# Block 1's linear attention: five levels and the diagonal as 32x32 blocks in a compact area

## The reference

```python
def gla_chunk_scan(q, k, v, log_g, state0, with_output):
    ...
    def step(state, inp):
        qc, kc, vc, gc = inp
        b = jnp.cumsum(gc.astype(jnp.float32), axis=2)
        ...
        diff = jnp.where(lower_tri, b[:, :, :, None, :] - b[:, :, None, :, :], -jnp.inf)
        a = jnp.einsum('bhtk,bhsk,bhtsk->bhts', qc, kc, jnp.exp(diff))
        o = (jnp.einsum('bhts,bhsv->bhtv', a, vc)
             + jnp.einsum('bhtk,bhkv->bhtv', qc * jnp.exp(b), state))
        return new_state, o
```

## Time and profile before

| what | value |
|---|---|
| median of three runs | 2466.95 us |
| span of the profiled execution | 2469.0 us |
| PE, PEld busy | 97%, 83% |
| DVE, ACT busy | 73%, 60% |
| layer 0: first diagonal product to first out-projection product | 219.47 to 268.36 us |
| layer 1: the same | 817.13 to 847.79 us |
| mean granted clock of PE | 0.993 |

### The profile page before, as it was taken

How to read it: one execution, slowest core, us unless ns; L and a number is a source line. 1 busy time by engine, 2 the same in 40 slices (tenths; PEclk the granted TensorE clock), 3 DMA queues, 4 the chain that set the end, 5 groups by cost and what they waited for, 6 DMA issues and landing times.

```text
span 2469.0 us, 38577 instructions
## 1 busy us (share of the span) xinstructions
PE 2402.1 (97%) x15096; PEld 2048.9 (83%) x15096; DVE 1803.2 (73%) x2445; ACT 1478.9 (60%) x1940; POOL 27.0 (1%) x86
## 2 busy tenths in 40 slices
PE   8999999999999899999999999999999999999998
PEld 6876788888887688898888889898888888888886
DVE  5556666566566666676666657579898898898997
ACT  4255366465444556556665545667777777777775
POOL 0000000000000000010000001000000000000000
PEclk9999999999999999999999999999999999999999
DMA  8236245555544545554235545147998998999996
GB/s 340 103 145 258 111 156 189 189 185 189 186 162 148 230 177 188 188 181 154 89 142 197 188 171 198 69 154 271 372 358 338 370 359 339 368 361 351 360 359 255
DMA packets 81640, 564.58 MB, mean 229 GB/s; under 512 B 9328, under 2 KB 12672, under 8 KB 13632
## 3 DMA queue, kind: packets, MB, share of 16 engines
q1 hardware_dynamic: 80144, 559.97, 60.6%
q0 software_dynamic: 1328, 2.25, 0.3%
HBM read 559.97 MB, written 1.05 MB: 227 GB/s over the span
## 4 chain that ended last, share of the span: by engine, by line
PE 88%; DVE 5%; ACT 4%; issue 1%; DMA 1%; SPq 0%; DVEq 0%; ACTq 0%
PE psum L247 86%; DVE ring_lo L241 2%; ACT ring_hi L238 2%; PE psum L740 1%; PE psum L2518 1%; DMA ring<-in_stream 1%; DMA Z<-in_first_mods 1%; ACT hT L793 1%; DVE hT L829 1%; ACT Z L801 0%; ACT turned_probs L801 0%; DVE hT L1533 0%; DVE Z L1465 0%; DVE mixT L647 0%; DVE hT L444 0%
## 5 line engine op out<-in xcount | busy, mean ns | idle before, releaser
L241 DVE TENSOR_TENSOR ring_lo<-ring,ring_hi 128x2048 fp32r<-128x2048 f32 x477 | 1092.2, 2291 | 272.7 <-ACT ring_hi L238 266.9
L238 ACT ACTIVATE ring_hi<-ring 128x2048 fp32r<-128x2048 f32 x477 | 912.4, 1914 | 334.1 <-PE psum L247 327.8
L247 PE MATMUL psum<-h_parts,ring_hi 128*128 128x512 f32 (+1 forms) x3184 | 861.2, 350 | 8.4 <-DVE h_parts L454 4.1
L247 PE MATMUL psum<-h_parts,ring_lo 128*128 128x256 f32 (+1 forms) x2464 | 601.6, 291 | 0.0
L247 PEld LDWEIGHTS psum<-h_parts,ring_hi 128*128 128x128 f32 x3184 | 515.8, 190 | 34.4 <-issue 10.5
L247 PE MATMUL psum<-ring_hi,h_parts 128*128 128x512 f32 (+1 forms) x1920 | 534.6, 365 | 0.4 <-ACT tok L324 0.4
L247 PEld LDWEIGHTS psum<-h_parts,ring_lo 128*128 128x128 f32 x2464 | 466.6, 189 | 72.5
L247 PEld LDWEIGHTS psum<-ring_hi,h_parts 128*128 128x128 f32 x1920 | 338.6, 189 | 52.6 <-ACT tok L324 0.8
L247 PE MATMUL psum<-ring_lo,h_parts 128*128 128x512 f32 (+1 forms) x960 | 347.5, 362 | 0.0
L247 PE MATMUL psum<-ring_hi,Zr 128*128 128x512 f32 (+1 forms) x736 | 225.3, 388 | 0.0
L247 PEld LDWEIGHTS psum<-ring_lo,h_parts 128*128 128x128 f32 x960 | 181.0, 189 | 28.8
(11 more groups left out here) (305 smaller groups left out, 2078.7 us busy)
## 6 DMA issues: line engine op xcount, KB each, us to landing
ring<-in_stream SPq DMA_DIRECT2D x524, 1024.0 KB, 4.8
Z<-in_first_mods SPq DMA_DIRECT2D x5, 1024.0 KB, 16.9
cst<-in_constants SPq DMA_DIRECT2D x1, 1216.0 KB, 7.9
mixT<-mixT POOLq DMA_DIRECT2D x32, 35.5 KB, 4.0
xT<-in_xT SPq DMA_DIRECT2D x1, 1024.0 KB, 6.2
xT<-in_ctxT SPq DMA_DIRECT2D x1, 1024.0 KB, 8.5
xT<-in_memT POOLq DMA_DIRECT2D x1, 1024.0 KB, 8.7
out_y<-hT SPq DMA_DIRECT2D x4, 256.0 KB, 2.5
```

Of the source, the lines that this page charges most:

```text
L238: e.activation(hi, raw, ACT.Copy).then_inc(sem("piece_rounded"), 1)
L241: e.tensor_tensor(lo, raw, hi.bitcast(F32), ALU.subtract).then_inc(sem("piece_split"), 1)
L247: ins = pe.matmul(*args, **kw)
```

## The change

Diagonal and levels 0 to 4 no longer multiply 128 by 128 but only the four 32x32 blocks on the diagonal of each tile and head (all that these five levels want lies there): 16 products of 32 keys by 32 queries for a tile instead of four. The results lie side by side in 64 columns of two banks for each tile, in turn in banks 2, 3 and 4, 5. DVE takes a level of all tiles and heads with one masked copy, 128 by 512 elements in layer 0 and 128 by 256 in layer 1, into a compact area `gA_blocks`, after the merges of that level. Levels 5 and 6 are multiplied as before, in banks 0 to 3; ACT copies them whole into `gA`, two tiles (one in layer 1) after each half of level 6; then DVE places the blocks over them, four copies of 32 partitions for each half. The merges of level 6 no longer have copies between them. `pe_gla_out` waits for all of this before its products with the values. ACT's split of two pieces comes after its copies of level 6. The masks shrink from 7x128 to 5x32 columns, and `other_w` gets memory of its own, so that POOL loads it without waiting for `keys_decayed`.

```diff
-        lvl_mask = sb("lvl_mask", [P, LEVELS, P], U8)
-        other_w = sb("other_w", [P, DEPTH, TAPS], over="lvl_mask")
+        lvl_mask = sb("lvl_mask", [P, BLOCK_LEVELS, BLOCK], U8)
+        other_w = sb("other_w", [P, DEPTH, TAPS])
...
+        gA_blocks = hflat[:, 2048:2560].rearrange("p (u w n) -> p u w n", u=2, n=BLOCK)
...
+        def pe_blocks(pe, i, tiles, keys_at, queries_at):
+
+            for t in tiles:
+                for c in range(2):
+                    at = 256 + (2 * t + c) * BLOCK
+                    for a in range(0, P, BLOCK):
+                        for u in range(2):
+                            r = slice(u * HD, (u + 1) * HD)
+                            mm(pe, bank[block_banks(i) + u][a:a + BLOCK, at:at + BLOCK],
+                               keys_at[r, c, t * P + a:t * P + a + BLOCK], queries_at(t, r, c, a), start=True, stop=True,
+                               last_of="grams" if (t, c, a, u) == (tiles[-1], 1, P - BLOCK, 1) else None)
+
         def pe_gla_levels(pe, layer):
...
+            for tiles in halves_of(nt):
+                pe_blocks(pe, 0, tiles, GK, lambda t, r, c, a: GQ[r, c, t * P + a:t * P + a + BLOCK])
+            phase_others(pe)
+            for l in range(BLOCK_LEVELS):
+                if l:
+                    pe.wait_ge(sem("gram_read"), rd + l)
+                for tiles in halves_of(nt):
+                    await_next(pe, "level_keys" if l else "level")
+                    pe_blocks(pe, l + 1, tiles, keys_now if l else GK, lambda t, r, c, a: queries_now(l, t, r, c, a))
                 for m in in_level(layer, l):
                     pe_mod_add(pe, layer, 1, m)
+            advance(pe, "level", 4 * (BLOCK_LEVELS - 1))
+            pe.wait_ge(sem("gram_read"), rd + BLOCK_LEVELS)
+            for l in range(BLOCK_LEVELS, LEVELS):
+                for tiles in halves_of(nt):
+                    await_next(pe, "level", 2)
+                    for t in tiles:
+                        pe_direct(pe, l, t, nt, t == tiles[-1])
...
         def act_gla_levels(act, layer):
...
-            for t in range(nt):
-                act.wait_ge(sem("grams"), gr + t + 1)
-                act.activation(by_bank(t), grams(t), ACT.Copy, scale=2.0).then_inc(sem("gram_read"), 1)
+            act.wait_ge(sem("grams"), gr + 2)
+            act.activation(blocks_kept(nt), block_grams(0, nt), ACT.Copy, scale=2.0).then_inc(sem("gram_read"), 1)
...
             act_rows_sum(act, layer, 1)
+            for part, tiles in enumerate(halves_of(nt)):
+                act.wait_ge(sem("grams"), gr + 2 * LEVELS + part + 1)
+                for t in tiles:
+                    act.activation(by_bank(t), grams(t, nt), ACT.Copy).then_inc(sem("gram_read"), 1)
...
         def dve_gla_levels(dve, layer):
...
             for l in range(LEVELS):
                 for part in range(2):
-                    for t in order[part]:
-                        dve.wait_ge(sem("grams"), gr + nt * (l + 1) + t + 1)
-                        if MASKED - 1 <= l < LEVELS - 1:
-                            continue
-                        dve.wait_ge(sem("gram_read"), own + (nt * l + t + 1 if l < MASKED else nt * MASKED))
-                        dve.copy_predicated(by_bank(t), mask, grams(t)).then_inc(sem("gram_read"), 1)
+                    dve.wait_ge(sem("grams"), gr + 2 * (l + 1) + part + 1)
                     dve_merge(dve, layer, l, part).then_inc(sem("level" if l < LEVELS - 1 else "keys_decayed"), 1)
+                if l < BLOCK_LEVELS:
+                    await_next(dve, "gram_read")
+                    mask = lvl_mask[:, l, :].unsqueeze(1).unsqueeze(1).to_broadcast([P, 2, 2 * nt, BLOCK])
+                    dve.copy_predicated(blocks_kept(nt), mask, block_grams(l + 1, nt)).then_inc(sem("gram_read"), 1)
...
+            for part, tiles in enumerate(halves_of(nt)):
+                dve.wait_ge(sem("gram_read"), own + (part + 1) * len(tiles) + part)
+                for a in range(0, P, BLOCK):
+                    r, w = slice(a, a + BLOCK), slice(2 * tiles.start, 2 * tiles.stop)
+                    out = gA[r, tiles.start:tiles.stop, :, a:a + BLOCK].rearrange("p t (v u) n -> p u (t v) n", u=2)
+                    ins = dve.tensor_copy(out, gA_blocks[r, :, w, :])
+                ins.then_inc(sem("gram_read"), 1)
...
             turn(0)
             turn(1)
+            await_next(pe, "gram_read", len(outs) + 2)
             within(outs[0:2])
...
-            pool.wait_ge(sem("keys_decayed"), 5)
             pool.dma_start(other_w[:, :, :], A["other_taps"]).then_inc(sem("taps_in"), 16)
```

More of the change, by code:

```diff
@@ L82 @@
 LEVELS = 7
+BLOCK = 32
+BLOCK_LEVELS = 5
 N_FIRST = CONST["pair"][1]
@@ L1324, in gla_level, with gram, grams, block_banks @@
             return x[:, :, :, 0, :], x[:, :, :, 1, :]
[L1328 to L1333, removed]
+        def gram(t, h, nt):
+            half, within = divmod(t, nt // 2)
+            return bank[2 * half + h % 2][:, (2 * within + h // 2) * P:(2 * within + h // 2 + 1) * P]
+        def grams(t, nt):
+            half, within = divmod(t, nt // 2)
+            at = slice(2 * within * P, 2 * (within + 1) * P)
+            return psum[:, 2 * half:2 * half + 2, at].rearrange("p u (v n) -> p u v n", v=2)
         def by_bank(t):
             return gA[:, t].rearrange("p (v u) n -> p u v n", v=2)
+        def block_banks(i):
+            return 2 + 2 * (i % 2)
+        def block_grams(i, nt):
+            b = block_banks(i)
+            return psum[:, b:b + 2, 256:256 + nt * 2 * BLOCK].rearrange("p u (w n) -> p u w n", n=BLOCK)
+        def blocks_kept(nt):
+            return gA_blocks[:, :, 0:2 * nt, :]
+        def halves_of(nt):
+            return range(0, nt // 2), range(nt // 2, nt)
         def in_level(layer, l):
@@ L1343, in pe_gla_levels @@
         def pe_gla_levels(pe, layer):
-            tiles = range(4 if layer == 0 else 2)
+            nt = 4 if layer == 0 else 2
             rd = base(pe, "gram_read")
[L1346 to L1373, removed]
-                        continue
[L1375 to L1379, removed]
@@ L1385, in build, with pe_direct @@
-        MASKED = 5
-        def pe_direct(pe, l, t):
+            await_next(pe, "gram_read", 1 + BLOCK_LEVELS)
+        def pe_direct(pe, l, t, nt, last):
             w = 1 << l
@@ L1394, in pe_direct, with queries_now @@
                         r = slice(u * HD, (u + 1) * HD)
-                        mm(pe, gram(t, 2 * c + u)[a:a + w, b:b + w], gK[d][r, c, t * P + a:t * P + a + w],
+                        mm(pe, gram(t, 2 * c + u, nt)[a:a + w, b:b + w], gK[d][r, c, t * P + a:t * P + a + w],
                            gQ[d][r, c, t * P + b:t * P + b + w], start=True, stop=True,
-                           last_of="grams" if (c, a, u) == (1, blocks[-1][0], 1) else None)
+                           last_of="grams" if last and (c, a, u) == (1, blocks[-1][0], 1) else None)
         def by_halves(x, l):
             return x.rearrange("p c (b u h) -> p c b u h", u=2, h=1 << l)
-        def queries_now(l, t, r, c):
+        def queries_now(l, t, r, c, a):
             h = 1 << l
-            first = Zt[r, c, t * P:(t + 1) * P]
+            first = Zt[r, c, t * P + a:t * P + a + BLOCK]
             (step, n), _ = first.ap
-            return bass.AP(first.tensor, first.offset, [[step, n], [2 * h, P // (2 * h)], [20 * 2 * T + h, 2], [1, h]])
+            return bass.AP(first.tensor, first.offset, [[step, n], [2 * h, BLOCK // (2 * h)], [20 * 2 * T + h, 2], [1, h]])
         def act_level_keys(act, layer, l, part):
@@ L1514, in dve_levels_ahead @@
             return step
-        def halves_of(nt):
-            return range(0, nt // 2), range(nt // 2, nt)
         def dve_gla_levels(dve, layer):
@@ L1540, in dve_gla_levels @@
                     ins.then_inc(sem("keys_decayed"), 1)
-            advance(dve, "grams", nt * (1 + LEVELS))
-            advance(dve, "gram_read", nt * (1 + MASKED))
+            await_next(dve, "gram_read")
+            own = base(dve, "gram_read")
+            for part, tiles in enumerate(halves_of(nt)):
[5 more added lines that the diff above has]
+                ins.then_inc(sem("gram_read"), 1)
+            advance(dve, "gram_read", nt + 2)
+            advance(dve, "grams", 2 * (1 + LEVELS))
             heads, levels = IN_HEADS[layer], IN_LEVELS[layer]
@@ L3165, in constants @@
         out[:, a:b] = c[name]
-    lv = np.zeros((P, LEVELS, P), np.float32)
-    s, q = r[:, None], r[None, :]
-    for l in range(LEVELS):
+    lv = np.zeros((P, BLOCK_LEVELS, BLOCK), np.float32)
+    s, q = r[:, None] % BLOCK, np.arange(BLOCK)[None, :]
+    for l in range(BLOCK_LEVELS):
         same = (s >> (l + 1)) == (q >> (l + 1))
         lv[:, l] = same & (((s >> l) & 1) != ((q >> l) & 1))
-    lv[:, 4] = (s >> 4) != (q >> 4)
     return out, lv.reshape(P, -1)
```

13 lines of the change are left out of this document (4 added, 9 removed).

## The result

The changed kernel takes 2479.26 us (median of five, 2478.49 to 2483.94) against 2466.95 us: a ratio of 1.0048, 95% interval 1.0037 to 1.0059, so 9 to 15 us slower. The prediction was 2480. The profiled execution has a span of 2478.5 us.

A forecast was written before the change was run, and what follows sets the result against it. PE, busy 97% of the span, was taken as the bound, starving on instruction packets. 10.8 - 1.3 + 1.1 + 2.7 = +13.3 us on the profiled 2469.0, with the median 2 us under it, gave 2480; range 2460 to 2489.

The forecast's parts named there:

- The one stall of 1.64 us: PE's wait by "issue" at 250.31 us, mid level 5 of layer 0, before the change; read as instructions run dry.
- Layer 0, +10.8: Layer 0, to the end of level 6: PE waits for instruction packets, level 6 ends at 264.0 instead of 253.2.
- Eight turns at 5.4: Layer 0's levels: PE steps into a next instruction packet that is not ready eight times, 5.4 us each.
- the ends of 4.5 and 6.0: Lowest and highest us for PE's step to an instruction packet not ready; +2.5 and +20.5 us on the whole kernel.
- DVE in the levels, nothing: DVE's 4.9 us a level become 3.0, wholly beside PE's wait for packets: no change in time.
- The end of layer 0, -1.3: After layer 0's level 6: merges come first, value products wait 4.3 us instead of 5.65; ends +0.8 and -2.4.
- The form without a row: DVE's 32x256 block copies after level 6, not in the profile: 0.34 us each, 2.7 us for eight.
- ACT in layer 1, +1.1: Layer 1's state products wait for ACT's turned keys, queued behind the splits: 5.1 us after level 6 instead of 4.0.
- the third rival: PE starved stays at the lower clock into layer 0's out-projection: up to 3 us more, 2483; within the slower case's 0.72.
- Layer 1, +2.7: Layer 1, to the end of level 6: four more packet waits, level 6 ends at 841.2 instead of 838.5.
- Packets in time: Rival: PE keeps several instruction packets, the stream bounds next; -6.4 us, 2460.5 us; chance 0.13.
- Turns at 4.5 us or less: Rival: each step to the next instruction packet is at its cheapest, +2.5 us or less, 2469 us; chance 0.15.

The follow-up runs named there:

- the kernel with three quarters left out: The changed kernel without three quarters of its block products in the diagonal and levels 0 to 4: 2460.60 us, ratio 0.9967 to the kernel before.

## Why the prediction was right, point by point

**What bounds.** The one stall of 1.64 us was read as PE running dry of a packet, and all that follows rests on it. It held: 256 instructions from stall to stall, a packet begun 2.2 to 2.7 us before PE goes on, and the five kernels in which the count was changed. The prediction's 250 a packet was 256. The Trainium skill, "Runtime: NRT & Kernel Launch", section "Instruction fetch mechanics", has blocks of 256 instructions, and there the trace agrees; that crossing from one to the next is mostly hidden holds in the kernel with 64x64 blocks (two stalls, 1.6 us) and not in the changed one (seven, 16.3 us).

**Layer 0, +10.8; measured +10.6.** The agreement is closer than the working. Eight turns at 5.4 were summed; from the first stall's end (221.38) to where PE turns into the ninth packet (261.94, in level 6, without a stall) the eight took 40.6 us, 5.07 each, 2.6 less in all. The first turn was taken as free, 1.1 us into the stretch; it stalled for 2.33 us and came 3.3 us into it. The two errors nearly cancel, and that is luck. Of the turns that ended in a stall the first, with the stream idle, took 4.0 us, the others 4.65 to 6.13: the ends of 4.5 and 6.0 were drawn about right, for a stretch under the stream.

**DVE in the levels, nothing.** A level's four merges and one copy take 3.2 us (230.52 to 233.69) where 3.0 were worked out, and DVE waits 28 us for PE: covered, as said.

**The end of layer 0, -1.3; measured -1.9.** The form without a row, a copy of 32x256, takes 0.30 us:

```profile
263.71 2.39 DVE L1555 COPY hT<-hT 32x256 f32<-32x256 f32 x8
```

2.4 us for all, 2.7 were taken. The transposes come 1.5 us after level 6 (1.4), the value products 3.7 (4.3), and the wait on the placement is 0.27 us. ACT's turned keys (267.07) are in time for the state products (268.93), hidden as argued.

**ACT in layer 1, +1.1; measured +1.5 to the state products, +2.3 to the out-projection.** The size came near by luck; the step did not happen. ACT's copy of the turned keys ended 5.2 us after level 6 (854.68), 5.1 were worked out, but PE did not wait for it: at a granted clock of 0.50 it was busy all the way to the state products at 5.5 us. Transposes and products with values took 5.05 us there instead of 2.84; that they began 0.66 us sooner after level 6, without copies between the merges, left +1.5. At the clock of before PE would have been there 3.3 us after level 6 (an estimate: 0.8 to the transposes, then the 2.54 of before), and by that estimate ACT would then have held it, as it does by 0.63 us in the kernel with 64x64 blocks. The lower clock was the third rival, up to 3 us, put into layer 0's out-projection; there the products take their 0.39, and it showed in layer 1's end instead.

**Layer 1, +2.7; measured +3.6.** The count held: four turns. The term that was mis-sized is their length: the 256 instructions that end at 828.77 began at 825.1, so the four took 22.4 us to 847.57 instead of 21.6, the first 3.6 and then 6.6 (828.77 to 835.40, DMA share 0.93) and 12.2 for two, above the end of 6.0; and what follows the last took 1.9 us instead of 1.4, at the lower clock.

**The sum.** +13.3 on the median came out at +12.3. In the profiled executions the four parts came to +14.6 and the span to +9.5, with -5.1 us in places that the change doesn't touch; carrying the span's 2 us over to the median hid that the span of before was the longer one of its kind.

**Rivals.** Packets in time: the next bound that it names, the stream, is what shows once the count is low, in the kernel with three quarters left out; its condition was not met in the changed kernel. That its 2460.5 us is also the 2460.6 of that kernel is luck: it was worked out for four times the products and from 2466.95, -6.4, where that kernel is 8.4 below 2469.03; and level 4 starts 3.4 us sooner by its own rows (243.16 to 239.8), not 3.2. Turns at 4.5 us or less: only without the stream, 3.45 to 4.02.

## What to carry to other kernels

Cutting a product into smaller ones takes PE's time down and its instructions up; ask first how long 256 instructions last (here each product is four of them), and where that is under 4 to 6 us for several packets in a row, count the packets and not the products. A single stall by "issue" in the middle of a run of like instructions, with an instruction packet begun 2 to 3 us before it ends, is the sign that the next such edit will starve. Then take the coarsest blocks that keep the shorter work of the other engines: 64x64 instead of 32x32 turned a loss of 0.5% into a gain of 0.2%.

## What the runs showed of the hardware

That a turn has a price even when no other transfer runs, 3.45 us for 256 instructions that take 1.9 us or less to work off, was not expected; nor that a turn with enough slow work in it passes without a stall (225.40 to 235.53 holds two turns, 10.1 us, and one stall of 1.36). And starving can be paid twice: the matmuls behind a row of stalls ran at the lower granted clock, which cost 0.2 us for each of twelve in the out-projection of one kernel and 2.2 us in the transposes and products with values of layer 1 in another.
